# Byte offsets of the split weights and of the low activations in a two-layer encoder kernel

## Time and profile before

| | us |
|---|---|
| median of 3 runs | 828.78 |
| lowest and highest | 828.54 to 829.38 |
| the profiled execution, own time | 827.36 |
| its span, first to last instruction | 825.5 |
| TensorE (PE) busy | 816.9 |
| VectorE (DVE) busy | 645.5 |
| ScalarE (ACT) busy | 450.7 |
| GpSimd (POOL) busy | 229.0 |

### The profile page before, as it was taken

How to read it: one execution, slowest core, us unless ns; L and a number is a source line. 1 busy time by engine, 2 the same in 40 slices (tenths; PEclk the granted TensorE clock), 3 DMA queues, 4 the chain that set the end, 5 groups by cost and what they waited for, 6 DMA issues and landing times.

```text
span 825.5 us, 13848 instructions
## 1 busy us (share of the span) xinstructions
PE 816.9 (99%) x5628; PEld 754.9 (91%) x5628; DVE 645.5 (78%) x1098; ACT 450.7 (55%) x590; POOL 229.0 (28%) x107
## 2 busy tenths in 40 slices
PE   9999999999999999999999999999999999999996
PEld 9998899889998899888888999999999999998885
DVE  7579785797659784798788978999999997656651
ACT  7756643546436643556544465465555557694432
POOL 0300000000000000002000009988989987680000
PEclk9999999999999999999999999999999999999999
DMA  9987566536764566535655666655655665549602
GB/s 329 395 293 268 175 203 221 186 121 204 234 187 143 172 210 218 179 102 186 222 180 181 201 206 203 203 175 186 204 190 176 197 203 175 185 155 354 201 4 102
DMA packets 99665, 163.68 MB, mean 198 GB/s; under 512 B 3600, under 2 KB 40720, under 8 KB 99096
## 3 DMA queue, kind: packets, MB, share of 16 engines
q1 hardware_dynamic: 98128, 160.64, 58.3%
q10 hardware_dynamic: 1480, 2.25, 0.7%
HBM read 160.76 MB, written 3.69 MB: 199 GB/s over the span
## 4 chain that ended last, share of the span: by engine, by line
PE 82%; DVE 13%; ACT 2%; issue 2%; DMA 0%; ACTq 0%; DVEq 0%
PE ps_acc L1259 16%; PE ps_acc L1256 16%; PE ps_acc L1258 16%; PE ps_acc L1242 9%; PE ps_acc L1244 9%; PE ps_acc L1245 9%; DVE sb_w_lo L823 5%; DVE sb_zT L1012 3%; ACT sb_w_hi L474 1%; PE ps_acc L1300 1%; PE ps_acc L1307 1%; PE ps_acc L1304 1%; DVE sb_mT L975 1%; DVE sb_probs L943 1%; DVE sb_conv_lo L1020 1%
## 5 line engine op out<-in xcount | busy, mean ns | idle before, releaser
L474 ACT ACTIVATE sb_w_hi<-sb_w_raw 128x2048 fp32r<-128x2048 f32 x139 | 265.9, 1921 | 226.0 <-PE ps_acc L1259 154.3
L446 POOL TENSOR_TENSOR sb_w_lo<-sb_w_raw,sb_w_hi 128x2048 fp32r<-128x2048 f32 x45 | 208.3, 4634 | 388.5 <-ACT sb_w_hi L474 388.4
L823 DVE TENSOR_TENSOR sb_w_lo<-sb_w_raw,sb_w_hi 128x2048 fp32r<-128x2048 f32 x94 | 213.7, 2290 | 92.0 <-ACT sb_w_hi L474 91.6
L1256 PE MATMUL ps_acc<-sb_conv_hi,sb_w_hi 128*128 128x256 f32 x768 | 213.2, 278 | 0.0
L1259 PE MATMUL ps_acc<-sb_conv_hi,sb_w_lo 128*128 128x256 f32 x768 | 212.1, 276 | 0.0
L1258 PE MATMUL ps_acc<-sb_conv_lo,sb_w_hi 128*128 128x256 f32 x768 | 212.1, 276 | 0.0
L1060 DVE SCALAR_TENSOR_TENSOR ps_d<-sb_uT,sb_dwT,ps_d 128x256 f32<-128x256 f32 x480 | 189.3, 524 | 4.5 <-ACT ps_d L704 4.5
L1242 PE MATMUL ps_acc<-sb_w_hi,sb_act_hi 128*128 128x512 f32 x384 | 149.7, 390 | 0.0
L1244 PE MATMUL ps_acc<-sb_w_lo,sb_act_hi 128*128 128x512 f32 x384 | 149.6, 390 | 0.0
L1245 PE MATMUL ps_acc<-sb_w_hi,sb_act_lo 128*128 128x512 f32 x384 | 149.4, 389 | 0.0
L1258 PEld LDWEIGHTS ps_acc<-sb_conv_lo,sb_w_hi 128*128 128x128 f32 x768 | 144.2, 188 | 0.1
(11 more groups left out here) (170 smaller groups left out, 878.4 us busy)
## 6 DMA issues: line engine op xcount, KB each, us to landing
sb_w_raw<-in_attn_w_in SPq DMA_DIRECT2D x59, 1024.0 KB, 5.8
sb_w_raw<-in_conv_w_in SPq DMA_DIRECT2D x64, 512.0 KB, 4.7
sb_w_raw<-in_attn_w_out SPq DMA_DIRECT2D x16, 1024.0 KB, 5.1
sb_w_raw<-in_conv_w_in SPq DMA_DIRECT2D x16, 1024.0 KB, 5.1
sb_w_raw<-in_conv_w_out SPq DMA_DIRECT2D x16, 1024.0 KB, 5.0
sb_w_raw<-in_attn_w_in SPq DMA_DIRECT2D x16, 256.0 KB, 4.3
sb_xs<-in_x SPq DMA_DIRECT2D x2, 1024.0 KB, 13.0
sb_x_in<-in_x_turned SPq DMA_DIRECT2D x15, 128.0 KB, 4.1
```

The lines of the kernel that those rows point to most:

```text
L446: pool.tensor_tensor(w_part(w_lo, c), w_raw[c % RING][:], w_part(w_hi, c).bitcast(F32), ALU.subtract).then_inc(lo_ready_pool, 1)
L474: act.activation(w_part(w_hi, c if like is None else like), w_raw[slot][:], ACT.Copy).then_inc(hi_ready, 1)
L823: dve.tensor_tensor(w_part(w_lo, like), w_raw[slot][:], w_part(w_hi, like).bitcast(F32), ALU.subtract).then_inc(lo_ready, 1)
L1256: pe.matmul(into, left_hi, hi[:, kt], start=(kt == 0 and f % 2 == 0), stop=False, skip_group_check=True)
```

## The change

The constants for the turned and the row form are replaced by a table for each stretch of the program: for each entry the shift in elements of the high part and of the low part. One element is 4 bytes, so 16, 32 and 48 stand for 64, 128 and 192 bytes. `act_lo` and `conv_lo` get a room that is 128 elements longer, in which they begin 32 elements (128 bytes) in. `act_hi` and `conv_hi` stay. What lies behind `act_lo` and `conv_lo` moves by 512 bytes, and no more than that.

```diff
--- before.py
+++ after.py
@@ -51,7 +51,13 @@
 VECS_AT, LAM_AT = 4, 8
 VEC_ROOM = 9 * KT + 4
 W_GAP = 128
-TURNED_AT, ROWS_AT, LOW_TURNED_AT = 32, 16, 0
+ACT_LO_AT = CONV_LO_AT = 32
+PAIR_TURNED_AT = ((32, 0), (0, 32), (0, 32), (0, 32))
+LAST_K_AT = (32, 32)
+PAIR_ROWS_AT = ((32, 32), (0, 0), (0, 0), (32, 0))
+OUT_AT = ((32, 32), (0, 0), (0, 32), (32, 0))
+CONV_AT = ((32, 0), (0, 32), (32, 32), (0, 0), (16, 48), (48, 16))
+CONV_OUT_AT = ((32, 32), (0, 0), (16, 48), (48, 48))
 Q_HI_AT, Q_LO_AT = 16, 48
 WARM_UP = 9
 POOL_FROM = CHUNKS_OUT + 2 * RING
@@ -77,6 +83,9 @@
     with ExitStack() as ctx:
         def sb(name, shape, dt=F32, scope=ctx):
             return scope.enter_context(nc.sbuf_tensor("sb_" + name, shape, dt))
+
+        def by_tile(room, at):
+            return room[:, at:at + KT * SEQ].rearrange("p (k s) -> p k s", s=SEQ)
 
         def psum(name, shape):
             return ctx.enter_context(nc.psum_tensor("ps_" + name, shape, F32))
@@ -121,7 +130,7 @@
 
         with ExitStack() as one:
             act_hi = sb("act_hi", [P, KT, SEQ], F32R, one)
-            act_lo = sb("act_lo", [P, KT, SEQ], F32R, one)
+            act_lo = by_tile(sb("act_lo", [P, KT * SEQ + W_GAP], F32R, one), ACT_LO_AT)
 
             with ExitStack() as start:
                 table = sb("table", [HEADS, BUCKETS], F32, start)
@@ -148,7 +157,7 @@
                 bias_w = sb("bias_w", [P, 2, BW], F32, two)
             with ExitStack() as two:
                 conv_hi = sb("conv_hi", [P, KT, SEQ], F32R, two)
-                conv_lo = sb("conv_lo", [P, KT, SEQ], F32R, two)
+                conv_lo = by_tile(sb("conv_lo", [P, KT * SEQ + W_GAP], F32R, two), CONV_LO_AT)
                 zT = sb("zT", [P, KT, SEQ], F32, two)
                 diag = sb("diag", [P, 2, SEQ], F32, two)
                 x1T = zT
@@ -300,8 +309,16 @@
 
         def place(c, low):
 
-            turned = c % 16 < 2 * NCH if c < CHUNKS_ATT else CHUNKS_OUT <= c < CHUNKS_CONV
-            return (LOW_TURNED_AT if low else TURNED_AT) if turned else ROWS_AT
+            if c >= CHUNKS_CONV:
+                return CONV_OUT_AT[(c - CHUNKS_CONV) // NCH][low]
+            if c >= CHUNKS_OUT:
+                return CONV_AT[(c - CHUNKS_OUT) // (2 * NCH)][low]
+            if c >= CHUNKS_ATT:
+                return OUT_AT[(c - CHUNKS_ATT) // NCH][low]
+            j, t = c // 16, c % 16 // NCH
+            if j == PAIRS - 1 and t == 1:
+                return LAST_K_AT[low]
+            return (PAIR_TURNED_AT if t < 2 else PAIR_ROWS_AT)[j][low]
 
         def pair_chunk(j, i):
```

## The result

The changed kernel is slower: 851.77 us, the median of four runs (851.64 to 851.91), against 828.66 us for the kernel before (four runs, 827.37 to 829.38). The ratio is 1.0281, with a 95% interval of 1.0269 to 1.0293. The forecast was 828.8 us, no change, and its range ended at 832.5.

The account below looks back on a forecast made before the run. TensorE's own stream of matmuls was taken as the bound. All terms of the change summed to 0: 827.4 us against the profiled execution, predicted as 828.8 us against the median, range 823.0 to 832.5 us.

Parts of the forecast that it names:

- What bounds the kernel: TensorE's own matmul stream sets the time, 805.1 of 813.8 us; no buffer, transfer or other engine holds it up.
- the test that it named: In the changed trace, a mid-stretch chunk differing from 5.44 us by more than 0.03 us makes the prediction wrong.
- Distances 0, 64 and 192: Next matmul's weights start less moving operand's start, modulo 256 bytes; at these three values it was claimed to cost nothing.
- The pairing: Compares one matmul's moving operand with the next one's weights, whose load starts within 0.01 us of that matmul.
- The moving start itself: Moving operands starting at 64, 0 or 128 instead of 192 modulo 256 bytes: taken as 0 cost.
- Distance 128: Last 8 conv-in chunks and last conv-out group: reads 128 bytes apart collide, 3.4 us, 832.2 us; slower in all 0.22.
- the restarts' 6.7 ns: Extra spacing of a 256-column matmul that doesn't start on time, 0.12 instead of 0.113 us, from rows around 61 us.
- The faster rival: Row stretches with moving weights at 0 or 128 return the 17/16 excess: 17.9 us, 810.9 us, or partly 823.7; chance 0.18.
- the lost cycle in 17: Every matmul spacing is 17/16 of one column per cycle: 6.7 ns lost at 256 columns, 13.3 at 512.
- the room: act_lo and conv_lo's space is 512 bytes longer, shifting what lies behind by a multiple of 256: nothing.
- the other engines: ScalarE's L474 differs by at most 1% between places, and its idle time covers more: 0 cost.

Follow-up runs that it names:

- The split matmuls: Kernel before with each row product split into two matmuls of 256 columns and output groups' weights at 192, 128, 0, 64: 848.49 us.
- the first kernel: Weights at the places of the kernel before, only act_lo and conv_lo moved 128 bytes further on: 859.81 us, ratio 1.0379 against the kernel before.

## Why the prediction was wrong

**What bounds the kernel** was read rightly, and the test that it named was the right one. The kernel takes as long as TensorE's stream, TensorE never waits, the clock is full, and the distance between starts accounts for the whole 24.6 us. The prediction called itself wrong if a chunk in the middle of a stretch left 5.44 us by more than 0.03; every chunk did.

**The failed step** is "*Distances 0, 64 and 192* are priced by the rows at nothing". Two readings went wrong in it. It pooled two forms: 0 had been seen under 512 columns alone, 64 and 192 under 256 alone. The text said so and still took all of them for free. The split matmuls show that the number of columns decides: 0 is free with 512 columns and costs 6.7 ns with 256; 64 is free with 256 columns and costs 6.7 ns with 512. And it read a price for a distance out of a mixture: 192 had only been seen as one of three, between two 64s. With all three at 192 a loose stream pays 4.4 ns. The 20 chunks of pairs 1 to 3 and the 8 of the second conv-in stretch, which the prediction had at 192 three times, take 5.65 us without a break, 4.4 ns a matmul: 28 x 48 x 4.4 ns = 5.9 us, over three times what a measurement can tell.

**The pairing** of one matmul's moving operand with the next one's weights was a choice from the weight load beside the matmul, and the runs don't bear it out as the whole story. By that pairing the first kernel has 64 for all three kinds, and so has the first conv-in stretch of the change; both are loose, at 5.79 us. It also has 0 for all three in the fifth conv-in stretch of the change and 128 in the sixth, and both take 5.65 us, no more than the second. One number per distance is shown only for streams in which every stationary and every moving operand have the same distance, so that any pairing gives the same.

**The moving start itself** ("I take 0, since a 1024-byte read passes through all four quarters of 256 bytes wherever it starts") failed as an argument. The reads do pass through all quarters, and where they stand relative to the other read still counts, down to 4 bytes. That the start by itself is free turned out true: 64 bytes for all cost nothing.

**Distance 128** was the slower rival: 832.2 us. Its mechanism, two reads of TensorE that collide at some distances, is the nearest to what happened, and with 256 columns its price had the right size: the restarts' 6.7 ns against 5.3 measured; with 512 it was 13.3 against 5.7. What failed was its place. I gave it 448 matmuls, and nearly all of the 5184 turned and row matmuls paid, 16.5 us over 3648 turned ones (4.5 ns each) and 7.5 us over 1536 row ones (4.9 ns each), while the last 8 conv-in chunks, for which it said 5.76 us, take 5.65 like those before them. A term of 3.4 us was 24.6. The restart rows also held a hint that I read only as a price: 0.12 us is what the matmuls behind a break keep for two to ten starts in the kernel before, and what loose streams keep for good.

**The faster rival** fell. In none of the fourteen kernels does a chunk take less than 5.44 us: none of the places tried brings the lost cycle in 17 back. The rule of the Trainium skill that the prediction set beside it (TensorE: Matmul & The Clock Gate, section Back-to-back issue gap; the page gives it for a single isolated matmul) makes 109.2 and 215.8 ns; 113.33 and 226.67 are the least that any place gave.

**Right at nothing** were the room (512 bytes, and 256 bytes for the low activations: 0.9995), the other engines (ScalarE's high part 1915 ns on average, VectorE and GpSimd as busy as before), and that TensorE doesn't begin to wait for them.

**Open** is which two reads meet. The weight load beside a matmul is the nearest candidate, since the spacing is lost with the other engines idle, but no run took the load away, and the loads' own records didn't grow (188 ns on average in both kernels) while those of the matmuls did, from 278 to 282 ns (L1256, L1273) and from 390 to 394 (L1242, L1259). A matmul's end is modelled in the profile, so that says little by itself. Open also is why a mixture is not the mean of its parts (16.1 and 31.6 us give 23.1), and what lets a stream recover at some places and not at others. DMA into the same memory ran in every kernel, and no run is without it; it carries the same bytes in the packed kernels.

No version beat the kernel before. The two that equal it, low activations at +256 and all at +64 bytes, lie within 0.1% of it.

## What to carry to other kernels

Where a stream of matmuls is back to back, read the distance between starts, not busy time, and look how it recovers behind a break. In this kernel the starts of the stationary and moving operands modulo 256 bytes belong together: move all of them by the same amount, or by multiples of 256, and treat the number of columns as part of the choice. A price read from the trace holds for the form, the size and the neighbours under which it was seen. Before taking a quantity for free, fix all others: three distances that were taken as free under both sizes were in truth two free combinations out of eight.

## What the hardware showed that I had not expected

TensorE can be slowed by where its own operands start, by 1% to 7% per matmul (228.9 against 226.67 ns, 120.9 against 113.33), with no wait in the trace, the clock at 1.00 and VectorE, ScalarE and GpSimd idle (234 instead of 226.67 ns at 835.8 us of the changed kernel). The page SBUF — State Buffer of the Trainium skill, section Who interferes with whom, gives TensorE two independent read ports, for the moving operand and the weight load, and has it wait on no one. The trace agrees in that the kernel before keeps 113.33 ns while ScalarE and GpSimd work. But with the relative start of the two operands the spacing went from 113.33 to 120.9 ns. If it is these two reads that meet, which stays open, they are not independent in speed; there the measurement decides.

The stream has two lasting spacings at the same places: 113.33 and 118.8 ns on either side of four transposes in one stretch. And the effect is sharp: in the row form +4 bytes off the good place cost more than +64 (5.71 and 5.49 us against 5.44), though -4 bytes cost little (5.48).
